# Second mixer of a two-block network: value matrices as stationary operand, three attention branches summed in one PSUM bank

## The chip, the core and the metric

One NeuronCore of a Trainium2 chip runs the whole network for a sequence of 256 tokens of width 2048, batch 1. The time is the device time of one execution in microseconds (us). TensorE (PE), VectorE (DVE), ScalarE (ACT), GpSimd (POOL) and SyncE (SP) each run their own list of instructions in order and wait for each other by semaphores.

## The reference

A first block (pooling and stick-breaking attention, then a feed-forward part) is followed by two mixers. The change is in the last one, `mixer_b`; the first mixer of the pair, `mixer_a`, ends with the same `(o * silu(z)) @ w_out`.

```python
def mixer_b(h, w_in, ..., w_out, cos, sin):
    q, kc, vc, ks, vs, kw, vw, gates, z = jnp.split(h @ w_in, cuts, axis=-1)
    kcmp, vcmp = compress(kc, ...), compress(vc, ...)              # 15 compressed keys and values
    o_cmp, o_slc = nsa_cmp_slc(q, kcmp, vcmp, ks, vs)              # two of the three branches
    o_win = banded_attention(q, kw, vw, B_WINDOW, WIN_QBLOCK)      # the third
    g = jax.nn.sigmoid(gates).reshape(Bn, S, 3, B_KV_GROUPS, B_GROUP, 1)
    o = g[:, :, 0] * o_cmp + g[:, :, 1] * o_slc + g[:, :, 2] * o_win
    return (o.reshape(Bn, S, B_WIDTH) * jax.nn.silu(z)) @ w_out
```

There are 4 key groups of 8 heads with 64 numbers each. At 256 tokens the selected and the window branch both see every earlier token, so both are plain causal softmax attention, with different keys and values.

## The kernel before

Every large product (256 x 2048 times 2048 x N) streams its weights in chunks of 512 columns. One step is one block of 128 rows of a chunk: six matmuls of 512 columns (`mm_tile`, L625 to L627; two token tiles, and three products each, since weights and activations are split into a high and a low fp32r part). The parts are made two steps at a time by `cast` (ACT, L1163, `w_high`) and `rest` (DVE, L1676, `w_low`), three such halves ahead of PE, into rings of four.

The attention rides on this stream. Stage "b" is the list of steps of `b_z` and `b_q` of the four groups and of `b_out`; group g starts at step 32 g, and what hangs on a step stands ahead of that step's six matmuls on PE and ahead of that step's cast and rest on ACT and DVE. Within a group the work goes in eight pairs of heads (pairs 0 to 3 in the selected branch, 4 to 7 in the window branch). Pair i has these pieces, counted in steps from the group's start:

- `pair_scores` (PE, step 8 + 3 i): eight small matmuls into banks 0 and 1.
- `pair_mask` (DVE, same step): adds the mask, two maxima, and the negated maximum.
- `pair_exp` (ACT, step 10 + 3 i): four exponentials, each followed by a read of its row sum.
- `pair_turn` (PE, step 13 + 3 i): six transposes of the weights into banks 1 and 2. It waits until what these banks held has been read.
- `pair_store` (ACT, same step, and ahead of the exponentials that stand on it): one copy of the transposed weights from banks 1 and 2 to `pt`.
- `pair_values` (PE, at the turn of the next pair; for pair 7 at step 37): the transposed weights are the stationary operand and 64 columns of values stream, six matmuls per pair, into bank 3.
- `add_outputs` (DVE, after every second pair): reciprocal of the row sums, times the gate, times the bank (512 columns), added to `oo`.

The compressed branch has its own pieces: `cmp_scores` (PE, step 5), `cmp_shift` and `cmp_weights` (DVE, steps 5 and 7), `cmp_turn` (step 10), and `cmp_values` (PE, step 12), two matmuls of 512 columns into banks 2 and 3 with which `oo_begin` (DVE) starts `oo`. After the last pair `oo_gate` multiplies `oo` by silu(z), and at step 40 (`OO_STEP`) `oo_turn` makes eight transposes on PE, `turn_high` and `turn_low` (L1307 on ACT, L1917 on DVE) split them into `DHI` and `DLO`, the stationary operand of `b_out`.

Stage "a" is the first mixer. It already runs in the form that the change brings to "b": `head_values` (L955, L957) has the values as stationary operand, `z_turn` transposes silu(z) through bank 2, `z_store` (L1488) copies it to `zT`, and `out_gate`, `out_high`, `out_low` finish two heads at a time. It has one pair per six steps.

The scores of a pair write bank 1, so they wait until the turn of two pairs before has been stored:

Of the kernel before, what the change touches and what calls it, by code (L numbers as in the profile page):

```python
# [7 lines left out]
F32 = mybir.dt.float32  # L8
# [5 lines left out]
P = 128  # L14
# [47 lines left out]
    "outputs": ("weights_scaled", "z_turned", "z_stored", "out_gated", "out_high", "out_low", "outputs_read", "branch_added", "rd_step", "oo_gated"),  # L62
# [170 lines left out]
OO_STEP = 40  # L233

Z_STEPS = (18, 23)
# [17 lines left out]
def gate_step(i):  # L253

    return value_step("a", i) + 1
# [15 lines left out]
def body(nc, t, ctx, known):  # L271
# [333 lines left out]
    def tensor_program(T):  # L605
# [298 lines left out]
        def pair_scores(name, g, i, k_):  # L904
# [4 lines left out]
            for tt in range(NT):  # L909
                c0, n = (0, P) if tt == 0 else (P, SEQ)  # L910
                for e in range(2):
                    o = e * HD
                    mm = T.matmul(bank(e)[:, c0:c0 + n], qG[o:o + HD, i % 4, tt * P:(tt + 1) * P], k_[o:o + HD, 0:n],  # L913
                                  start=True, stop=True)
# [15 lines left out]
        def pair_values(name, g, i, vals):  # L930
            if i % 2 == 0:
                T.wait_ge(*emptied[3])
            T.wait_ge(*of("pt_made", (name, g, i)))
            v0, v1 = (vals[:, tt, g * HD:(g + 1) * HD] for tt in range(2))
            for e in range(2):
                s, c0 = 2 * (i % 2) + 1 - e, (2 * (i % 2) + e) * HD
                o0, o1 = bank(3)[:, c0:c0 + HD], bank(3)[:, SEQ + c0:SEQ + c0 + HD]
# [3 lines left out]
            mm.then_inc(*done("valued", (name, g, i)))  # L941
            if i % 2 == 1:
                emptied[3] = of("outputs_read", (name, g, i // 2))

        def oo_turn(g):
            for half in range(2):
                T.wait_ge(*of("oo_gated", ("b", g, half)))
                turn_half("oo_b", g, oo, half, 2)

        def head_values(g, i):  # L950
            T.wait_ge(*emptied[3])
            T.wait_ge(*of("pt_made", ("a", g, i)))
            v0, v1 = (va[:, tt, g * HD:(g + 1) * HD] for tt in range(2))
            for e in range(2):
                T.matmul(bank(3)[e * HD:(e + 1) * HD, 0:SEQ], v0, pt[:, 2 * (i % 2) + 1 - e, 0:SEQ], start=True, stop=False)  # L955
# [1479 lines left out]
```

## Time and profile before

| | us |
|---|---|
| median of 3 runs | 2270.18 |
| lowest and highest run | 2269.04 and 2273.67 |
| the profiled execution, its own time | 2271.82 |
| span of that execution, first to last instruction | 2270.5 |
| PE busy, share of the span | 97% |
| DVE busy, ACT busy | 64%, 48% |

A profile gives start, duration, engine, line and tiles of each instruction, and what an engine was waiting for. The end of a matmul is modelled and reaches into the next one; how much TensorE time a piece takes is read from the starts on both sides of it. A row of a timeline merges equal neighbours ("x6"), and an fp32 matmul that isn't a transpose shows as two records. The engines ACT and DVE begin an instruction while the last part of the one before still runs, so their cost in a row is also the distance of starts.

### The profile page before, as it was taken

What the parts mean: (1) busy time and instruction counts of PE and PEld (TensorE: products, weight loads), DVE (VectorE), ACT (ScalarE), POOL (GpSimd) and SP (SyncE); (2) the same over time, 40 slices, a digit from 0 to 9 for tenths busy, and PEclk for the clock granted to TensorE, in tenths of its full rate; (3) what the DMA queues carried; (4) which work ended last, traced back from release to release, by engine and by line L of the source; (5) the groups of instructions that cost most, each with busy time, mean ns of one, the idle gap of its engine ahead of it and who ended that gap; (6) DMA issues with size and microseconds to landing.
All of it is one profiled execution on the core that took longest, in us unless ns stands there. A gap on an engine that the chain in (4) does not pass through costs nothing.

```text
span 2270.5 us, 27331 instructions
## 1 busy us (share of the span) xinstructions
PE 2206.2 (97%) x10659; PEld 1803.4 (79%) x10659; DVE 1463.9 (64%) x1919; ACT 1078.8 (48%) x1599; POOL 175.9 (8%) x318
## 2 busy tenths in 40 slices
PE   6889999999998999999999999999999999999998
PEld 5777788888887888888888888877778877877777
DVE  6767878888875566565554456566665536666664
ACT  3234356544446534444443544555555524565544
POOL 0004311122210000000000000000000000000000
PEclk8889999999998999999999999999999989999999
DMA  9997866788885677777555555544445633333333
GB/s 344 331 305 271 302 206 230 252 307 304 305 288 164 228 238 238 229 237 226 185 185 192 179 193 178 186 149 149 149 154 185 215 123 126 107 112 113 110 130 130
DMA packets 242165, 468.53 MB, mean 206 GB/s; under 512 B 14363, under 2 KB 52469, under 8 KB 241397
## 3 DMA queue, kind: packets, MB, share of 16 engines
q1 hardware_dynamic: 213552, 387.74, 51.9%
q0 software_dynamic: 20480, 67.13, 8.7%
q10 hardware_dynamic: 8004, 11.93, 1.5%
q8 instruction: 85, 1.39, 0.2%
q14 instruction: 44, 0.35, 0.0%
HBM read 464.65 MB, written 2.10 MB: 206 GB/s over the span
## 4 chain that ended last, share of the span: by engine, by line
PE 88%; DVE 5%; issue 2%; ACT 2%; DMA 2%; POOL 1%; SPq 0%; ACTq 0%; DVEq 0%
PE banks L625 26%; PE banks L627 25%; PE banks L626 25%; PE banks L637 2%; PE banks L913 2%; PE banks L925 1%; DVE ada_acc_vec L1735 1%; DMA ada_w<-in_w_ada 1%; ACT w_high L1163 1%; DVE w_low L1676 1%; PE banks L940 1%; PE banks L939 1%; PE banks L1028 1%; PE banks L938 1%; DVE ada_acc L1696 1%
## 5 line engine op out<-in xcount | busy, mean ns | idle before, releaser
L1676 DVE TENSOR_TENSOR w_low<-raw,w_high 128x1024 fp32r<-128x1024 f32 x674 | 821.9, 1224 | 625.7 <-ACT w_high L1163 625.2
L1163 ACT CAST w_high<-raw 128x1024 fp32r<-128x1024 f32 x674 | 701.4, 1046 | 791.4 <-PE banks L627 791.1
L625 PE MATMUL banks<-w_high,act_a_high 128*128 128x512 f32 (+1 forms) x1696 | 691.2, 408 | 21.7 <-DVE act_a_low L1768 14.2
L626 PE MATMUL banks<-w_low,act_a_high 128*128 128x512 f32 (+1 forms) x1696 | 668.3, 394 | 0.0
L627 PE MATMUL banks<-w_high,act_a_low 128*128 128x512 f32 (+1 forms) x1696 | 668.1, 394 | 0.0
L625 PEld LDWEIGHTS banks<-w_high,act_a_high 128*128 128x128 f32 x1696 | 326.6, 193 | 103.9 <-issue 21.6
L627 PEld LDWEIGHTS banks<-w_high,act_a_low 128*128 128x128 f32 x1696 | 326.3, 192 | 69.5
L626 PEld LDWEIGHTS banks<-w_low,act_a_high 128*128 128x128 f32 x1696 | 326.6, 193 | 63.1 <-issue 2.4
L625 PE MATMUL banks<-w_high,act_b_high 128*128 128x512 f32 x640 | 250.7, 392 | 0.0
L627 PE MATMUL banks<-w_high,act_b_low 128*128 128x512 f32 x640 | 249.1, 389 | 0.0
L626 PE MATMUL banks<-w_low,act_b_high 128*128 128x512 f32 x640 | 249.0, 389 | 0.0
L509 POOL DMA_DIRECT2D ada_w<-in_w_ada x256 | 139.7, 546 | 709.6 <-DVE ada_acc L1696 614.2
L1696 DVE SCALAR_TENSOR_TENSOR ada_acc<-ada_w,cT,ada_acc 128x512 f32<-128x512 f32 x240 | 179.4, 747 | 15.6 <-DMA ada_w<-in_w_ada 12.5
L626 PEld LDWEIGHTS banks<-w_low,act_b_high 128*128 128x128 f32 x640 | 120.2, 188 | 25.1 <-issue 0.5
L627 PEld LDWEIGHTS banks<-w_high,act_b_low 128*128 128x128 f32 x640 | 120.1, 188 | 25.1
L625 PEld LDWEIGHTS banks<-w_high,act_b_high 128*128 128x128 f32 x640 | 120.2, 188 | 25.0 <-issue 0.5
L1471 ACT ACTIVATE scores<-scores,minus_max 128x128 f32<-128x128 f32 x192 | 85.0, 448 | 8.2 <-DVE minus_max L2099 6.7
L1482 ACT COPY ada_w<-banks 128x768 f32<-128x768 f32 x48 | 38.4, 800 | 94.2 <-PE banks L925 94.2
L1735 DVE SCALAR_TENSOR_TENSOR ada_acc_vec<-ada_first,cT,ada_acc_vec 128x512 f32<-128x512 f32 x88 | 66.0, 750 | 4.1 <-DMA ada_first<-in_w_ada 1.8
L625 PE MATMUL banks<-w_high,act_d_high 128*128 128x512 f32 x128 | 51.4, 401 | 1.6 <-DVE act_d_low L1917 1.6
L625 PE MATMUL banks<-w_high,act_c_high 128*128 128x512 f32 x128 | 50.9, 398 | 0.0
L627 PE MATMUL banks<-w_high,act_d_low 128*128 128x512 f32 x128 | 50.0, 391 | 0.0
(338 smaller groups left out, 2013.5 us busy)
## 6 DMA issues: line engine op xcount, KB each, us to landing
raw<-in_w_ff SPq DMA_DIRECT2D x128, 1024.0 KB, 5.2
raw<-in_w_in SPq DMA_DIRECT2D x64, 1024.0 KB, 7.0
ada_w<-in_w_ada POOLq DMA_DIRECT2D x256, 256.0 KB, 4.8
raw<-in_b_w_in SPq DMA_DIRECT2D x44, 1024.0 KB, 5.1
raw<-in_a_w_in SPq DMA_DIRECT2D x36, 1024.0 KB, 5.1
ada_first<-in_w_ada SPq DMA_DIRECT2D x64, 512.0 KB, 9.0
raw<-in_w_o SPq DMA_DIRECT2D x16, 1024.0 KB, 7.1
raw<-in_a_w_out SPq DMA_DIRECT2D x16, 1024.0 KB, 5.2
```

Source lines behind the costliest of these rows:

```text
L509: G.dma_start(ada_w[:, u % ADA_RING, :], t["w_ada"][0, q * P:(q + 1) * P, col:col + AC]).then_inc(*landed(f"ada_landed{u % ADA_RING}", u))
L625: T.matmul(out, xh, wh, start=(c.first and k == 0), stop=False)
L626: T.matmul(out, xh, wl, start=False, stop=False)
L627: last = T.matmul(out, xl, wh, start=False, stop=(c.last and k == c.nk - 1))
L637: tr = T.transpose(bank(b)[:, j * SEQ + tt * P:j * SEQ + (tt + 1) * P], src[:, tt, c0 + j * P:c0 + (j + 1) * P], ident[:, :])
L913: mm = T.matmul(bank(e)[:, c0:c0 + n], qG[o:o + HD, i % 4, tt * P:(tt + 1) * P], k_[o:o + HD, 0:n], start=True, stop=True)
L1163: A.copy(WH[:, h % SPL, :, :], split_ap(h)).then_inc(*done("high", h))
L1471: A.activation(sc[:, s, c0:c0 + n], sc[:, s, c0:c0 + n], ACT.Exp, scale=R, bias=nm[:, i // 4, j, tt:tt + 1], accum_out=sm[:, i // 4, j, tt ...
L1482: A.copy(pt[:, 2 * (i % 2):2 * (i % 2) + 2, :], banks[:, 5:7, 0:3 * P]).then_inc(*done("pt_made", (name, g, i)))
L1676: V.tensor_tensor(WL[:, h % SPL, :, :], split_ap(h), WH[:, h % SPL, :, :].bitcast(F32), ALU.subtract).then_inc(*done("low", h))
L1696: V.scalar_tensor_tensor(out=acc_, in0=w, scalar=c_, in1=acc_, op0=ALU.mult, op1=ALU.add).then_inc(*done("ada_acc", u))
L1735: V.scalar_tensor_tensor(out=acc_, in0=w, scalar=c_, in1=acc_, op0=ALU.mult, op1=ALU.add).then_inc(*done("first_vec", (i, u, kk)))
```

## The change

The output of a pair of heads is now built transposed, in bank 3, for all three branches: the compressed branch first (`vbd` stationary, 256 columns of `cpt` moving), then the selected branch, then the window branch, by accumulation. For that the pairs alternate between the branches (pair 2 j selected, pair 2 j + 1 window), and each branch's weights are scaled by gate over row sum before they are transposed: `gate_factor` on DVE (reciprocal, product, and the first 128 columns of two heads), `pair_scale` on ACT (the other 256 columns of each head). `cmp_values`, `oo_begin`, `add_outputs`, `oo_gate` and the turn of `oo` go; z is transposed instead, at steps 18 and 21, and the outputs are gated and split two heads at a time. On DVE the mask of the next pair stands one step earlier, behind the factor. On ACT the exponentials stand one step earlier.

```diff
@@
-OO_STEP = 40
+EXP = {"a": 2, "b": 1}
+BRANCHES = {"a": 1, "b": 2}
-Z_STEPS = (18, 23)
+Z_STEPS = {"a": (18, 23), "b": (18, 21)}
@@ tensor_program
         def pair_turn(name, g, i):
             for b in (1, 2):
                 T.wait_ge(*emptied[b])
-            T.wait_ge(*of("weights_scaled" if name == "a" else "scores_exp", (name, g, i)))
+            T.wait_ge(*of("weights_scaled", (name, g, i)))
+            if name == "b":
+                T.wait_ge(*of("weights_wide", (name, g, i)))
@@
         def pair_values(name, g, i, vals):
-            if i % 2 == 0:
+            j, first, last = i // BRANCHES[name], i % BRANCHES[name] == 0, (i + 1) % BRANCHES[name] == 0
+            if first:
                 T.wait_ge(*emptied[3])
+            if first and name == "b":
+                T.wait_ge(*of("cpt_made", g))
+                T.matmul(bank(3)[:, 0:SEQ], vbd[0:HB, g, j * P:(j + 1) * P], cpt[0:HB, :, :].rearrange("p a n -> p (a n)"),
+                         start=True, stop=False)
...
-                T.matmul(o0, pt[:, s, 0:P], v0, start=True, stop=True)
-                T.matmul(o1, pt[:, s, P:2 * P], v0, start=True, stop=False)
-                mm = T.matmul(o1, pt[:, s, 2 * P:3 * P], v1, start=False, stop=True)
+                T.matmul(bank(3)[e * HD:(e + 1) * HD, 0:SEQ], v0, pt[:, 2 * (i % 2) + 1 - e, 0:SEQ],
+                         start=(name == "a"), stop=False)
+            for e in range(2):
+                mm = T.matmul(bank(3)[e * HD:(e + 1) * HD, P:SEQ], v1, pt[:, 2 * (i % 2) + 1 - e, 2 * P:3 * P],
+                              start=False, stop=last)
...
+        def z_turn(name, g, half):
+            T.wait_ge(*of("pair_free", (name + "_z", g)))
+            if emptied[2] is not None:
+                T.wait_ge(*emptied[2])
+            transposes(2, zs, 2 * half * P).then_inc(*done("z_turned", (name, g, half)))
+            emptied[2] = of("z_stored", (name, g, half))
@@ scalar_program
+        def pair_scale(g, i):
+            A.wait_ge(*of("rd_step", ("b", g, i, 1)))
+            for e in range(2):
+                w = sc[:, 2 * (i % 2) + e, P:3 * P]
+                A.activation(w, w, ACT.Copy, scale=rd[:, 2 * (i % 4) + e, 1:2]).then_inc(*done("weights_wide", ("b", g, i)))
@@ pair_hooks of ACT
+            for j in range(GH // 2):
+                if rel == gate_step(name, j):
+                    out_high(name, g, j, CHI if name == "a" else DHI)
...
+            for i in range(PAIRS[name]):
+                if rel == score_step(name, i) + EXP[name]:
+                    pair_exp(name, g, i)
+            for i in range(PAIRS[name]):
+                if name == "b" and rel == score_step(name, i) + 2:
+                    pair_scale(g, i)
             for i in range(PAIRS[name]):
                 if rel == turn_step(name, i):
                     pair_store(name, g, i)
-            for i in range(PAIRS[name]):
-                if rel == score_step(name, i) + 2:
-                    pair_exp(name, g, i)
-            if name == "a" and rel in Z_STEPS:
-                z_store(g, Z_STEPS.index(rel))
+            if rel in Z_STEPS[name]:
+                z_store(name, g, Z_STEPS[name].index(rel))
@@ vector_program
+        def gate_factor(g, i):
+            br, j, o, s = i % 2, 2 * (i // 2), 2 * (i % 4), 2 * (i % 2)
+            hs, g0 = slice(o, o + 2), 32 * (br + 1) + GH * g + j
+            V.wait_ge(*of("scores_exp", ("b", g, i)))
+            V.reciprocal(rd[:, hs, :], sm[:, br, j:j + 2, :]).then_inc(*done("rd_step", ("b", g, i, 0)))
...
+            V.tensor_tensor(rd[:, hs, :], rd[:, hs, :], gts[:, :, g0:g0 + 2].rearrange("p a h -> p h a"),
+                            ALU.mult).then_inc(*done("rd_step", ("b", g, i, 1)))
...
+            V.tensor_tensor(w, w, rd[:, hs, 0].unsqueeze(2).broadcast_to([P, 2, P]), ALU.mult).then_inc(*done("weights_scaled", ("b", g, i)))
@@
+                out_hooks("b", g, rel)
                 if rel == 5:
                     cmp_shift(g)
                 if rel == 7:
                     cmp_weights(g)
-                if rel == 12:
-                    oo_begin(g)
                 for i in range(PAIRS["b"]):
-                    if rel == score_step("b", i):
+                    if rel + 1 == score_step("b", i) + 2:
+                        gate_factor(g, i)
+                for i in range(PAIRS["b"]):
+                    if rel + 1 == score_step("b", i):
                         pair_mask("b", g, i, maskB)
```

What the built program holds on ACT for two pairs around step 16 of a group, before: the store (`ada_w<-banks`), then the exponentials of the pair, then the cast.

```order
L1521 ACTIVATE zs<-banks,inverse_rms 128x512 x2
L1482 COPY ada_w<-banks 128x768
L1471 ACTIVATE scores,row_sum<-scores,minus_max 128x128
L1471 ACTIVATE scores,row_sum<-scores,minus_max 128x256
L1471 ACTIVATE scores,row_sum<-scores,minus_max 128x128
L1471 ACTIVATE scores,row_sum<-scores,minus_max 128x256
L1163 CAST w_high<-raw 128x1024 x2
L1482 COPY ada_w<-banks 128x768
```

The same engine now, from the exponentials of pair 3 (step 18) to the store at step 22. L1449 are the exponentials, L1473 the copy of z, L1140 the cast, L1461 `pair_scale`, L1467 the store, L1477 `out_high`.

```order
L1449 ACTIVATE scores,row_sum<-scores,minus_max 128x256
L1473 COPY z_transposed<-banks 128x512
L1140 CAST w_high<-raw 128x1024
L1461 ACTIVATE scores<-scores,row_rec 128x256 x2
L1467 COPY ada_w<-banks 128x768
L1477 CAST act_d_high<-outputs_gated 128x256
L1140 CAST w_high<-raw 128x1024
L1449 ACTIVATE scores,row_sum<-scores,minus_max 128x128
L1449 ACTIVATE scores,row_sum<-scores,minus_max 128x256
L1449 ACTIVATE scores,row_sum<-scores,minus_max 128x128
L1449 ACTIVATE scores,row_sum<-scores,minus_max 128x256
L1473 COPY z_transposed<-banks 128x512
```

The store of pair i - 1 now stands behind the exponentials and the scaling of pair i; the copy of z stands behind the exponentials of pairs 3 and 4, and the second one also behind `out_high` and a cast.

On PE a turn with the values behind it read as follows, before:

```order
L925 MATMUL banks<-ident,scores 128x128 x6
L938 MATMUL banks<-b_values_win,ada_w 128x64
L939 MATMUL banks<-b_values_win,ada_w 128x64
L940 MATMUL banks<-b_values_win,ada_w 128x64
L938 MATMUL banks<-b_values_win,ada_w 128x64
L939 MATMUL banks<-b_values_win,ada_w 128x64
L940 MATMUL banks<-b_values_win,ada_w 128x64
```

And now, where a new pair of heads begins (L940 is the compressed branch, at every second pair):

```order
L929 MATMUL banks<-ident,scores 128x128 x6
L940 MATMUL banks<-ada_w,gate_b 128x256
L945 MATMUL banks<-ada_w,b_values_sel 64x256 x2
L948 MATMUL banks<-ada_w,b_values_sel 64x128 x2
```

On DVE, at steps 19 to 21: mask and maxima of pair 4, then the gating of the first two heads, the rest, the low part, and the factor of pair 4.

```order
L2077 TENSOR_TENSOR scores<-banks,mask_causal 128x768
L2080 TENSOR_REDUCE row_max<-scores 128x2
L2081 TENSOR_REDUCE row_max<-scores 128x2
L2088 TENSOR_SCALAR minus_max<-row_max 128x4
L2100 TENSOR_TENSOR outputs_gated<-banks,z_transposed 128x256
L1662 TENSOR_TENSOR w_low<-raw,w_high 128x1024
L2107 TENSOR_TENSOR act_d_low<-outputs_gated,act_d_high 128x256
L2316 RECIPROCAL row_rec<-row_sum 128x4
L2318 TENSOR_TENSOR row_rec<-row_rec,b_gates 128x4
L2322 TENSOR_TENSOR scores<-scores,row_rec 128x2x128
```

The gating on DVE stands behind a mask that waits for scores, so `out_high` on ACT, and the exponentials behind it, come after that mask too.

## Rows read from the trace of the kernel before

**Rows 1.** The page: busy time by engine.
```profile
PE 2206.2 (97%) x10659; PEld 1803.4 (79%) x10659; DVE 1463.9 (64%) x1919; ACT 1078.8 (48%) x1599; POOL 175.9 (8%) x318
```

**Rows 2.** Stretches: length, busy us (x instructions) by engine, granted clock, DMA share, GB/s.
```profile
1994.12:2071.34 77.22, 76.52 (x456) 60.95 (x455) 51.58 (x89) 42.41 (x102) 0.00 (x0) 0.98 0.35 109
...
2047.80:2051.20 3.40, 3.40 (x46) 3.27 (x44) 1.23 (x1) 0.00 (x0) 0.00 (x0) 1.00 0.54 152
2051.20:2054.60 3.40, 3.40 (x8) 2.64 (x9) 3.16 (x11) 0.95 (x2) 0.00 (x0) 0.51 0.66 252
```

**Rows 3.** Waits of PE, from 1750 us on: us in total, times, longest.
```profile
PE banks L925 <- issue: 2.7, 4, 1.1
PE banks L625 <- DVE act_d_low L1917: 1.6, 1, 1.6
PE banks L938 <- DVE ada_acc L2338: 1.4, 3, 0.5
```

**Rows 4.** Timeline of PE around a turn and values in "b": start, us.
```profile
1921.07 0.39 PE L627 MATMUL banks<-w_high,act_a_low 128*128 128x512 f32 x1
...
1921.95 0.33 PE L938 MATMUL banks<-b_values_sel,ada_w 128*128 128x64 f32 x2
...
1923.53 0.39 PE L626 MATMUL banks<-w_low,act_a_high 128*128 128x512 f32 x1
```

**Rows 5.** Timeline of PE around a turn and values in "a".
```profile
1502.20 0.39 PE L627 MATMUL banks<-w_high,act_a_low 128*128 128x512 f32 x1
...
1503.17 0.65 PE L955 MATMUL banks<-ada_w,gate_b 128*64 128x256 f32 x4
...
1504.31 0.39 PE L626 MATMUL banks<-w_low,act_a_high 128*128 128x512 f32 x1
```

**Rows 6.** Timeline of PE: the records of one `cmp_values`.
```profile
1987.58 1.88 PE L1127 MATMUL banks<-gate_b,ada_w 120*128 120x512 f32 x4
```

**Rows 7.** Timeline of PE: scores, the next turn, the next scores.
```profile
1994.12 0.93 PE L913 MATMUL banks<-mask_window,qG 64*128 64x128 f32 x8
...
1997.86 0.82 PE L925 MATMUL banks<-ident,scores 128*128 128x128 f32 x6
...
2001.34 0.93 PE L913 MATMUL banks<-mask_window,qG 64*128 64x128 f32 x8
```

**Rows 8.** Timeline of DVE: the mask that waited for the first of these scores.
```profile
1995.10 0.96 DVE L2091 TENSOR_TENSOR scores<-banks,mask_causal 128x768 f32<-128x768 f32 x1 [1.38 <-PE banks L913]
...
1997.14 0.17 DVE L2102 TENSOR_SCALAR minus_max<-row_max 128x4 f32<-128x4 f32 x1
```

**Rows 9.** Timeline of ACT: a store, the exponentials of a pair, a cast.
```profile
2027.62 0.80 ACT L1482 COPY ada_w<-banks 128x768 f32<-128x768 f32 x1 [3.38 <-PE banks L925]
2028.32 0.41 ACT L1471 ACTIVATE scores<-scores,minus_max 128x128 f32<-128x128 f32 x1
...
2030.08 1.03 ACT L1163 CAST w_high<-raw 128x1024 fp32r<-128x1024 f32 x1
```

**Rows 10.** Timeline of ACT: the tanh of z.
```profile
1998.06 1.27 ACT L1521 ACTIVATE zs<-banks,inverse_rms 128x512 f32<-128x512 f32 x2 [1.72 <-PE banks L627]
```

**Rows 11.** Groups of ACT in stage "a", 1500 to 1690 us: busy us, mean ns.
```profile
L1492 ACT CAST act_c_high<-outputs_gated 128x256 fp32r<-128x256 f32 x14 | 5.7, 409 | 17.9 <-DVE outputs_gated L2126 17.9
...
L1488 ACT COPY z_transposed<-banks 128x512 f32<-128x512 f32 x6 | 3.5, 582 | 3.9 <-PE banks L637 3.9
```

**Rows 12.** Groups of DVE in stage "a", the same stretch.
```profile
L2126 DVE TENSOR_TENSOR outputs_gated<-banks,z_transposed 128x256 f32<-128x256 f32 x14 | 5.8, 417 | 0.0
```

**Rows 13.** Timeline of DVE: reciprocal and product of `add_outputs`; `cmp_weights` and what follows it.
```profile
1976.28 0.19 DVE L2332 RECIPROCAL row_rec<-row_sum 128x8 f32<-128x8 f32 x1
...
1976.71 0.69 DVE L2338 TENSOR_TENSOR ada_acc<-banks,gate_rec 128x512 f32<-128x512 f32 x1
...
1980.19 0.40 DVE L2317 TENSOR_REDUCE cmp_max<-ada_w 128x16 f32<-128x240 f32 x1
...
1981.65 1.28 DVE L1917 TENSOR_TENSOR act_d_low<-banks,act_d_high 128x512 fp32r<-128x512 f32 x2
```

More of the change, by code:

```diff
@@ L912, in pair_scores @@
                     o = e * HD
[L913 removed]
+                    mm = T.matmul(bank(e)[:, c0:c0 + n], qG[o:o + HD, i // BRANCHES[name], tt * P:(tt + 1) * P], k_[o:o + HD, 0:n],
                                   start=True, stop=True)
@@ L1120, in cmp_turn @@
             emptied[3] = of("cpt_made", g)
-        def cmp_values(g):
-            for b in (2, 3):
-                T.wait_ge(*emptied[b])
-            T.wait_ge(*of("cpt_made", g))
-            for tt in range(NT):
-                mm = T.matmul(bank(2 + tt), cpt[0:HB, tt, :], vbd[0:HB, g, :], start=True, stop=True)
-            mm.then_inc(*done("cmp_valued", g))
-            for b in (2, 3):
-                emptied[b] = of("oo_begun", (g, b - 2))
         for s, (c, k) in enumerate(stage_steps(C, "b")):
@@ L1482, in pair_store, with z_store, out_high @@
             A.copy(pt[:, 2 * (i % 2):2 * (i % 2) + 2, :], banks[:, 5:7, 0:3 * P]).then_inc(*done("pt_made", (name, g, i)))
[L1484 removed]
+        def z_store(name, g, half):
             if g > 0 and half == 0:
[L1486 to L1499 removed]
+                A.wait_ge(*of("out_gated", (name, g - 1, GH // 2 - 1)))
+            A.wait_ge(*of("z_turned", (name, g, half)))
+            A.copy(zT[:, 2 * half:2 * half + 2, :], two(bank(2))).then_inc(*done("z_stored", (name, g, half)))
+        def out_high(name, g, j, H):
+            A.wait_ge(*of("out_gated", (name, g, j)))
+            A.copy(H[:, GH // 2 * g + j, :], gated[:, j % 2, :]).then_inc(*done("out_high", (name, g, j)))
+        def pair_hooks(name, g, rel):
+            for j in range(GH // 2):
+                if rel == gate_step(name, j):
+                    out_high(name, g, j, CHI if name == "a" else DHI)
             if rel == 1:
@@ L2107, in silu @@
                                    op1=ALU.mult).then_inc(*done("pair_free", (name + "_z", g)))
-        def oo_gate(name, g, half, ready_):
-            cols = slice(SEQ * half, SEQ * (half + 1))
-            V.wait_ge(*of("pair_free", (name + "_z", g)))
-            V.wait_ge(*ready_)
-            for tt in range(NT):
-                V.scalar_tensor_tensor(out=oo[:, tt, cols], in0=oo[:, tt, cols], scalar=rh[:, tt:tt + 1], in1=zs[:, tt, cols],
-                                       op0=ALU.mult, op1=ALU.mult).then_inc(*done("oo_gated", (name, g, half)))
@@ new lines, in out_low, with out_hooks @@
+        def out_low(name, g, j):
+            H, L = (CHI, CLO) if name == "a" else (DHI, DLO)
+            k = GH // 2 * g + j
+            V.wait_ge(*of("out_high", (name, g, j)))
+            V.tensor_tensor(L[:, k, :], gated[:, j % 2, :], H[:, k, :].bitcast(F32),
+                            ALU.subtract).then_inc(*done("out_low", (name, g, j)))
+        def out_hooks(name, g, rel):
+            for j in range(GH // 2):
+                if rel == gate_step(name, j):
+                    out_gate(name, g, j)
+                if rel == gate_step(name, j) + 1:
+                    out_low(name, g, j)
@@ L2276, in vector_program @@
         V.wait_ge(*of("pair_free", ("b_gates",)))
-        V.tensor_scalar(gts[:, :, :], gts[:, :, :], 0.5, 0.5, ALU.mult, ALU.add).then_inc(*done("gates_made"))
+        V.tensor_scalar(gts[:, :, :], gts[:, :, :], 0.5, 0.5, ALU.mult, ALU.add).then_inc(*done("gates_made", 0))
+        V.wait_ge(*of("gates_made", 0))
+        for tt in range(NT):
+            V.tensor_scalar(gts[:, tt, :], gts[:, tt, :], rh[:, tt:tt + 1], None, ALU.mult).then_inc(*done("gates_made", 1))
+        V.wait_ge(*of("gates_made", 1))
         for k in range(KT):
```

134 lines of the change are left out of this document (30 added, 104 removed).

## The prediction

> **What bounds the kernel now.** The page comes first: PE is busy 97% of the span [rows 1]. Then the stretch from the first scores of one group of the second mixer to those of the next: 77.2 us, of which PE is busy 76.5 [rows 2]; the other two such stretches are 76.5 us each. DVE has work for two thirds of it and ACT for 55%. So time is gained by taking TensorE work away, and is lost wherever PE, which runs its list in order, meets something that isn't ready. The waits of PE say that it hardly ever does: 2.7 us before turns, 1.4 us before values and 1.6 us at the end of the stage, 5.7 us in 520 [rows 3]. The third question is how much room these waits have, since the change puts more work between a pair's scores and its stored weights.
>
> **What goes, on PE.** Values and turn in "b": from the last matmul ahead (1921.07) to the second one behind (1923.53) are 2.46 us; two stream matmuls of 0.227 are in that, so turn and values take 2.00 us, 0.65 of them the turn (1921.95 - 1921.07 - 0.23) [rows 4]. Stage "a" has the new form: 1504.31 - 1502.20 - 0.45 = 1.66 us [rows 5]. Per pair 0.34 us less; 32 pairs give 10.9 us. The compressed branch: four records of 512 columns per group [rows 6] become four matmuls, thus eight records, of 256 columns, the same number of columns: nothing. It might cost less or more by its weight loads; with half a record (0.2 us) either way per group that is 1 us in the range. The turn of `oo` (eight transposes) is replaced by two turns of z of four: nothing. The existing waits: before values, since bank 3 was read only after a reciprocal and a product (0.43 us [rows 13]) and a 0.69 us multiplication, now one of 0.42 [rows 12]; at the end of the stage, since the outputs of the last heads are split by step 39 and not at step 40; before the first turn of a group, since DVE no longer has two additions, two gatings and a split of 512 columns ahead of its mask. I take all 5.7 us [rows 3] and, since PE loses some 0.2 us more than the idle time shown when it is held up (the next weight load isn't under way), 1.7 us for the eight of them. **Gain: 10.9 + 5.7 + 1.7 = 18.3 us.**
>
> Outside PE: on DVE the factor (0.43 and one multiplication of 0.4) per pair replaces work of the same size per two pairs; on ACT two activations of 256 columns per pair are new. None shows in these rows at that size from SBUF; `out_high` is 0.41 for 256 columns [rows 11], of which about 0.1 overlaps the next, so 0.32 each, bounds 0.3 and 0.5. Neither engine gets full: ACT has for one pair 1.76 + 0.65 + 0.7 + 1.5 x 0.94 = 4.5 us of some 6.9.
>
> **What is put in the way.** I follow one pair. Zero is its first score matmul. DVE masks from 0.98 [rows 7, 8], the negated maximum is there at 3.2 (1997.14 + 0.17), and ACT is on the exponentials until 3.2 + 1.76 = 4.96 [rows 9]. The reciprocal and the product take until 5.5 [rows 13], scaling until 6.15, and only then comes the store of the pair before, 0.8 us [rows 9]: 7.0. The scores of the next pair write bank 1 and wait for that store. On PE they are due after 7.22 us as it was [rows 7], 0.34 less now, so at 6.87; where a new pair of heads starts, 0.43 later (the compressed matmul), at 7.3. Before the change the store stood ahead of the exponentials and was done soon after the turn, which had 3.5 us of room. Now the room is zero, and whatever stands between exponentials and store on ACT goes into PE:
>
> - scores of pair 2. The turn of pair 0 has no values behind it, so they are due at 3.74 + 0.65 + 1.38 = 5.8. On ACT a cast (0.94) comes between, and the mask of pair 1 is late by some 0.85, since it stands behind the factor of pair 0, and that pair's mask behind `cmp_weights` (1.46 us [rows 13]) and a rest. Store done at 7.0 + 0.94 - 0.45 (the cast covers the wait for the factor) + 0.85 = 8.2: **2.4 us**.
> - scores of pair 3: the tanh of z, 1.2 us [rows 10], less 0.5: 7.6 against 7.3: **0.3**.
> - turn of pair 2: bank 2 is held by the z turned at step 18, and `z_store` is behind the exponentials of pair 3: 4.96 + 0.58 [rows 11] + 0.05 = 5.6. The turn is due at 3.74 + 0.43 = 4.2 [rows 7]: **1.4**.
> - turn of pair 3, the same at step 21, but ACT first has `out_high`, which waits for a gating that DVE does behind the mask (3.1 + 0.4 = 3.5), then 0.32 and a cast of 0.94: the exponentials start at 4.8, the copy is done at 7.2, against 4.2: **3.0**.
> - scores of pair 6: a cast between: 7.4 against 6.87: **0.5**.
> - scores of pair 7: `out_high` and cast ahead of the exponentials as above, start 4.8; store done at 8.55 against 7.3: **1.25**.
>
> That is 8.85 us per group; in the first group DVE has nothing left from a group before, 0.8 us less. **Loss: 4 x 8.85 - 0.8 = 34.6 us.** Each of the 24 waits is known to some 0.3 us, bounds 28 and 42.
>
> [...]
>
> [...]
>
> **Sum.** Span 2270.5 - 18.3 + 34.6 + 3.0 = 2289.8. The profiled run's own time is 1.3 us above its span and 1.6 above the median, so the median to expect is 2270.2 + 19.3 = **2289 us**, 0.8% slower. What a measurement can tell from no change here is 0.2%, 4.5 us.
>
> **Rivals.**
> (B) Only the copies of z hold PE up; the scores don't wait. That needs a chain from scores to store shorter by 0.5 to 1 us, for instance if the scaling activations take far under 0.3 us. Then -18.3 + 4 x 4.4 = -0.7: 2269.5. Against it: the store's place on ACT is certain, and 7.0 against 6.87 leaves nothing.
> (C) PE hardly waits at all, the change gives its 18.3 us: 2252. For it: the profile of before has room on every engine. Against: z's copy is behind exponentials that can't begin before 3.2.
> [...]
> (E) The change doesn't save its 0.34 us per pair, since a full-width matmul (compressed branch) now comes between transposes and column-tiled values, and switching costs (1503.17 - 1502.97 = 0.2 us after the last transpose [rows 5]): gain 7 us instead of 18: 2300.
>
> **How the numbers follow.** Forecast (waits of both kinds) 0.58, its own range 2280 to 2298; B 0.12; C 0.09; D 0.13; E 0.08. Slower by over 0.2%: forecast, D, E: 0.79. Within 0.2%: B, 0.12. Faster: C, 0.09. The range takes in B and leaves out C below, and most of what is beyond D above: 2266 to 2305.
>
> **What would show it.** In the profile after: the values in the new form at 1.0 us per pair and no wait before values or at the end of the stage (gain right). Idle of PE before the transposes of the turn, ended by ACT's copy to `z_transposed`, eight times, about 17 us; idle of PE before score matmuls, ended by ACT's store, about 17 us, the longest 2.4 at pair 2 of each group (loss right). Distance from the first scores of a group to the next: about 81 us instead of 77. Wrong if the store is seen done before PE gets to the next scores: then the exponentials or the scaling are shorter than 1.76 and 0.65. Clock: drops near the turns of pair 3, more than one in stage "b".

## The result and the profile after

| | before | after |
|---|---|---|
| median of 4 runs each | 2269.6 | 2295.1 |
| lowest and highest run | 2268.8, 2273.7 | 2289.3, 2299.4 |
| profiled execution, its span | 2271.8, 2270.5 | 2297.2, 2295.9 |

The change makes the kernel slower: ratio 1.0104, interval 1.0088 to 1.0119. The forecast was 2289 us, 2266 to 2305. The four times of after lie 10 us apart, and go in the main with the mean granted clock of each run: 0.979 at 2299.4, 0.978 at 2297.2, 0.982 at 2293.0, 0.985 at 2289.3.

The page of after, busy time by engine:

```profile
PE 2204.0 (96%) x10547; PEld 1782.3 (78%) x10547; DVE 1459.1 (64%) x1953; ACT 1108.2 (48%) x1679; POOL 175.8 (8%) x318
```

PE has 112 records fewer than in [rows 1], yet its busy time fell by 2.2 us only. Where the rest went is seen in the stretch from the first scores of stage "b" to the last pair's scores, first of before, then of after (length, busy us by engine, granted clock, DMA share, GB/s):

```profile
1904.13:2183.97 279.84, 275.76 (x1648) 218.50 (x1647) 188.20 (x322) 155.86 (x379) 0.00 (x0) 0.99 0.34 110
```
```profile
1901.09:2212.39 311.30, 276.01 (x1553) 200.69 (x1553) 186.78 (x361) 184.30 (x457) 0.00 (x0) 0.96 0.30 99
```

The stretch grew by 31.5 us. PE is idle for 35.3 us of it where it was idle for 4.1, and its busy time stayed the same with 95 records fewer, since the mean clock is 0.96. After the last scores 3.0 us are gained (83.5 against 86.5), and the stage begins 3.0 us earlier (1901.1 instead of 1904.1) by things that the change doesn't touch, 1.7 of them since one low stretch of the clock (0.50) near 690 us was 3.4 us shorter in this execution. The waits of PE in after, from 1750 us on (us in total, times, longest):

```profile
PE banks L915 <- issue: 18.0, 14, 2.3
PE banks L929 <- issue: 16.8, 8, 2.9
...
PE banks L940 <- DVE outputs_gated L2100: 0.2, 1, 0.2
```

The three waits of [rows 3] are gone. L915 are the scores, L929 the transposes of the turn. "issue" names no releaser, so each kind has to be followed on ACT. The turn of pair 3 in the last group, on PE:

```profile
2187.44 0.60 PE L639 MATMUL banks<-ident,zs 128*128 128x128 f32 x4
...
2189.03 0.40 PE L629 MATMUL banks<-w_high,act_d_low 128*128 128x512 f32 x1
2192.36 0.84 PE L929 MATMUL banks<-ident,scores 128*128 128x128 f32 x6 [2.93 <-issue]
```

ACT at the same time:

```profile
2188.67 0.41 ACT L1477 CAST act_d_high<-outputs_gated 128x256 fp32r<-128x256 f32 x1 [4.39 <-DVE outputs_gated L2100]
2188.99 1.04 ACT L1140 CAST w_high<-raw 128x1024 fp32r<-128x1024 f32 x1
2189.93 0.40 ACT L1449 ACTIVATE scores<-scores,minus_max 128x128 f32<-128x128 f32 x1
...
2191.70 0.56 ACT L1473 COPY z_transposed<-banks 128x512 f32<-128x512 f32 x1
2192.23 0.91 ACT L1461 ACTIVATE scores<-scores,row_rec 128x256 f32<-128x256 f32 x2
2193.24 0.80 ACT L1467 COPY ada_w<-banks 128x768 f32<-128x768 f32 x1
```

and DVE, where the gating stands behind the mask that waited for the scores:

```profile
2186.07 0.96 DVE L2077 TENSOR_TENSOR scores<-banks,mask_causal 128x768 f32<-128x768 f32 x1 [2.03 <-PE banks L915]
...
2188.22 0.42 DVE L2100 TENSOR_TENSOR outputs_gated<-banks,z_transposed 128x256 f32<-128x256 f32 x1
```

z was transposed at 2187.44, but ACT stood waiting for VectorE's gating (4.39 us idle), then cast, then did the four exponentials, and copied z only at 2191.70; the turn starts 0.1 us after the copy's end. The scores of pair 2 wait for the store (L1467) in the same way; PE and then ACT, in the same group:

```profile
2162.96 0.82 PE L929 MATMUL banks<-ident,scores 128*128 128x128 f32 x6
...
2167.50 1.65 PE L915 MATMUL banks<-mask_window,qG 64*128 64x128 f32 x8 [2.33 <-issue]
```
```profile
2163.11 0.40 ACT L1449 ACTIVATE scores<-scores,minus_max 128x128 f32<-128x128 f32 x1 [0.73 <-DVE minus_max L2088]
...
2164.88 1.03 ACT L1140 CAST w_high<-raw 128x1024 fp32r<-128x1024 f32 x1
2165.82 0.90 ACT L1461 ACTIVATE scores<-scores,row_rec 128x256 f32<-128x256 f32 x2
2166.63 0.78 ACT L1467 COPY ada_w<-banks 128x768 f32<-128x768 f32 x1
```

Turned at 2162.96, stored at 2167.41, scores at 2167.50. And the eight score records take 1.65 us here, where those of [rows 7] take 0.93: the clock has fallen. Three low stretches of the clock, each at the end of a long wait or just behind it, and for comparison the two at and behind the wait of 2.93 us in the last group, where it didn't fall (2024.0 to 2027.4 is low too):

```profile
1938.60:1942.00 3.40, 3.40 (x14) 1.93 (x13) 0.00 (x0) 1.89 (x3) 0.00 (x0) 0.51 0.80 290
2020.60:2024.00 3.40, 2.75 (x10) 1.97 (x12) 0.77 (x3) 2.63 (x6) 0.00 (x0) 0.50 0.80 236
...
2082.10:2085.50 3.40, 3.40 (x13) 2.36 (x14) 1.80 (x3) 0.74 (x1) 0.00 (x0) 0.51 0.81 251
2189.40:2192.80 3.40, 0.47 (x5) 0.47 (x5) 2.32 (x5) 3.40 (x12) 0.00 (x0) 1.00 0.07 6
2192.80:2196.20 3.40, 3.40 (x24) 2.21 (x24) 0.00 (x0) 2.09 (x3) 0.00 (x0) 1.00 0.83 307
```

Busy for all 3.40 us, PE gets 13 or 14 records done at 0.51, and 24 at 1.00. The stage has about 24 us at the low level; before it had 3.4 [rows 2].

### The profile page after: what moved, and what is told of

Same layout as the page of the kernel before. It is cut to its first block, busy times and chain, and to the rows that moved or that the text cites. A ratio compares the mean times of both kernels' runs of the same rounds, so it can differ in the third digit from the quotient of the medians.

```text
span 2295.9 us, 27238 instructions
## 1 busy us (share of the span) xinstructions
PE 2204.0 (96%) x10547; PEld 1782.3 (78%) x10547; DVE 1459.1 (64%) x1953; ACT 1108.2 (48%) x1679; POOL 175.8 (8%) x318
## 4 chain that ended last, share of the span: by engine, by line
PE 83%; DVE 7%; issue 4%; ACT 3%; DMA 2%; POOL 1%; SPq 0%; ACTq 0%; DVEq 0%
PE banks L627 25%; PE banks L629 24%; PE banks L628 24%; PE banks L639 2%; PE banks L915 2%; DMA ada_w<-in_w_ada 1%; ACT w_high L1140 1%; DVE ada_acc_vec L1721 1%; DVE w_low L1662 1%; PE banks L929 1%; PE banks L945 1%; ACT scores L1449 1%; PE banks L1017 1%; SPq L470 0%; DVE ada_acc L1682 0%
## 5 line engine op out<-in xcount | busy, mean ns | idle before, releaser
L1140 ACT CAST w_high<-raw 128x1024 fp32r<-128x1024 f32 x674 | 701.6, 1046 | 769.7 <-PE banks L629 769.2
L627 PE MATMUL banks<-w_high,act_a_high 128*128 128x512 f32 (+1 forms) x1696 | 691.7, 408 | 20.5 <-DVE act_a_low L1754 13.4
L1449 ACT ACTIVATE scores<-scores,minus_max 128x128 f32<-128x128 f32 x192 | 85.0, 444 | 102.8 <-DVE minus_max L2088 68.0
L2077 DVE TENSOR_TENSOR scores<-banks,mask_causal 128x768 f32<-128x768 f32 x32 | 30.6, 955 | 58.8 <-PE banks L915 58.8
L929 PE MATMUL banks<-ident,scores 128*128 128x128 f32 x288 | 40.9, 279 | 17.5 <-issue 16.8
L929 PEld LDWEIGHTS banks<-ident,scores 128*128 128x128 f32 x288 | 34.4, 143 | 27.0 <-issue 22.3
```

Source lines behind the costliest of these rows:

```text
L627: T.matmul(out, xh, wh, start=(c.first and k == 0), stop=False)
L929: tr = T.transpose(bank(2 - e)[:, q * P:(q + 1) * P], sc[:, 2 * (i % 2) + e, q * P:(q + 1) * P], ident[:, :])
L1140: A.copy(WH[:, h % SPL, :, :], split_ap(h)).then_inc(*done("high", h))
L1449: A.activation(sc[:, s, c0:c0 + n], sc[:, s, c0:c0 + n], ACT.Exp, scale=R, bias=nm[:, br, j, tt:tt + 1], accum_out=sm[:, br, j, tt:tt + 1] ...
```

## The experiments

The theory: two kinds of wait, both made by the place of the exponentials on ACT (ahead of the store and of the copy of z) together with the longer chain from scores to scaled weights, and behind the longest of them a lower clock. Against it stand: the new form of the values costs the time (E); the order alone does; the waits are one lateness handed on; the low clock has nothing to do with the waits. Medians here are over 4 to 10 runs. The ratios are to before on the same chip; before itself took 2269.6 beside after and 2270.6 to 2271.9 beside the experiments, so a difference between two kernels that were timed on different chips is known to some 2 us.

**Store first.** The order part of the change undone on ACT; the values, the factor and the scaling stay.

```diff
-EXP = {"a": 2, "b": 1}
+EXP = {"a": 2, "b": 2}
@@ pair_hooks of ACT: pair_store now stands ahead of pair_exp
+                if rel == turn_step(name, i):
+                    pair_store(name, g, i)
+            for i in range(PAIRS[name]):
                 if rel == score_step(name, i) + EXP[name]:
                     pair_exp(name, g, i)
```

> The changed kernel with one part of the edit undone: in the second mixer ScalarE's list holds, for one step, the store of the pair turned before, then the exponentials, then the scaling, then the copy of z; the exponentials thus come a step later in the list than in the changed kernel. Nothing else differs. Theory (ScalarE's order makes the waits): no score waits for the store and the turn of pair 2 no longer waits, 16.8 us of waits before scores and 5.2 of the 18 before turns gone; the turn of pair 3 still waits for the second copy of z, about 1.2 us, four times. So 2295 - 17 - 5 - 7 (turns of pair 3) - some 7 of the lost clock = about 2258, range 2250 to 2265. Rival 1 (the column-tiled values and the change of width on TensorE cost the time, the waits are only where it shows): the time stays within 8 us of 2295. Rival 2 (the clock falls anyway, by the thin columns of turn and values): waits gone, but clock drops in the second mixer stay, about 2265 to 2270.

Measured: 2273.7 us (ratio 1.0014, 1.0005 to 1.0024): 21 us of the 25 are back, but it is 16 us above what was expected. The waits of its PE in the stage:

```profile
PE banks L929 <- issue: 9.4, 4, 2.4
PE banks L940 <- DVE outputs_gated L2100: 4.4, 7, 1.1
PE banks L929 <- DVE scores L2077: 1.2, 4, 0.3
```

All waits before scores are gone, and that of the turn of pair 2. The turn of pair 3 waits 2.35 us and not 1.2. ACT shows why, and the expectation had left it out:

```profile
1935.10 0.40 ACT L1477 CAST act_d_high<-outputs_gated 128x256 fp32r<-128x256 f32 x1 [3.14 <-DVE outputs_gated L2100]
1935.41 1.04 ACT L1140 CAST w_high<-raw 128x1024 fp32r<-128x1024 f32 x1
1936.35 0.58 ACT L1473 COPY z_transposed<-banks 128x512 f32<-128x512 f32 x1
```

No exponential stands here, but ACT still waits for the gating, which VectorE does after the mask of the next pair. The new second row is the same gating: bank 3 isn't free for the next compressed matmul (L940). Three low stretches of the clock, each at the turn of pair 3, remain (0.50 from 1938.50 to 1940.20 in the first). E isn't decided by this alone; the last kernels settle it.

**Copy of z first.** z_store ahead of the exponentials; nothing else.

```diff
         def pair_hooks(name, g, rel):
+            if rel in Z_STEPS[name]:
+                z_store(name, g, Z_STEPS[name].index(rel))
             ...
-            if rel in Z_STEPS[name]:
-                z_store(name, g, Z_STEPS[name].index(rel))
```

> The changed kernel, with ScalarE's copy of z moved ahead of the exponentials of the same step; nothing else differs. Theory: the turn of pair 2 no longer waits (5.2 us), the turn of pair 3 waits 1.2 instead of 2.9 us (6.8 us), the waits of the scores for the store stay at about 17 us or grow by up to 0.3 us each where the copy now stands ahead (pairs 3 and 4): 2295 - 12 - up to 5 of the clock + 2 = about 2280, range 2274 to 2286. If the waits of turns and scores were one and the same lateness handed on from one to the next, taking one kind away would leave the sum as it is, and the time would stay within 4 us of 2295.

Measured: 2282.8 us. Waits: 19.3 before scores (16 times), 4.6 before the turn (4 times, 1.2). As expected in both kinds: the turn's share can be taken away alone, while the scores' stays (1.3 us more). They are two waits, not one handed on.

**Waits filled.** Dummy matmuls from activations that are there, into bank 0, in the time of two of the waits.

```diff
         def pair_turn(name, g, i):
+            if name == "b" and i == 3:
+                T.wait_ge(*emptied[0])
+                fill(12)
@@ pair_scores
+            if name == "b" and i == 2:
+                T.wait_ge(*emptied[0])
+                fill(8)
```

> The changed kernel with dummy matmuls added, whose result nobody reads: in the second mixer TensorE does 8 matmuls of 512 columns into bank 0 just ahead of the scores of pair 2 and 12 just ahead of the turn of pair 3 of each group, in time in which it stood idle in the changed kernel (1.7 to 2.3 and 2.9 us). If such a matmul takes 0.22 us, 8 take 1.8 and 12 take 2.6 us. Theory (the clock falls behind these waits): with the waits filled the clock stays up there, the 9 us that the low clock costs in the second mixer shrink to at most 3, so 2287 to 2290, and the repeats lie closer together than the 10 us of the changed kernel. If the low clock is not tied to the idle time (but to the narrow columns behind it), 2295 or up to 4 us more.

Measured: 2288.8 us (2286.8 to 2289.1, 2.3 us apart), as expected: 80 matmuls more, and 6.2 us less. The same stretch as above, and one filled wait on PE:

```profile
1901.93:2204.22 302.29, 284.16 (x1633) 209.31 (x1633) 186.90 (x361) 184.31 (x457) 0.00 (x0) 1.00 0.31 101
```
```profile
2099.33 2.90 PE L926 MATMUL banks<-act_a_high 128*128 128x512 f32 x12
2102.43 0.85 PE L939 MATMUL banks<-ident,scores 128*128 128x128 f32 x6 [0.20 <-issue]
```

The clock is 1.00 throughout. In after the six transposes of that same turn took longer, with the clock at the low level:

```profile
2106.94 1.51 PE L929 MATMUL banks<-ident,scores 128*128 128x128 f32 x6 [2.91 <-issue]
```

So these low stretches are tied to PE standing idle there. Filling the waits gives back 6.2 us in the median; by the two profiled executions the stage is 9.0 us shorter (311.3 - 302.3).

**z turned together.** As "store first", and both halves of z at step 18, the first through bank 1, the second through bank 2.

```diff
-Z_STEPS = {"a": (18, 23), "b": (18, 21)}
+Z_STEPS = {"a": (18, 23), "b": (18,)}
@@ z_turn
-            if emptied[2] is not None:
-                T.wait_ge(*emptied[2])
-            transposes(2, zs, 2 * half * P)...
+            b = 2 if name == "a" else 1 + half
+            transposes(b, zs, 2 * half * P)...
```

> The changed kernel with the order of e1_store_first, and both halves of z turned at one step (18), the first into bank 1 and the second into bank 2, and copied together; pair 3 then finds both banks long free. Theory: no wait of TensorE above 0.2 us is left in the second mixer, and the gain of the values (0.34 us for each of 32 pairs, and most of the 5.7 us of old waits) is all there: 2252, range 2247 to 2257, faster than both kernels and some 5 us below e1_store_first. If two copies in a row on ScalarE push the exponentials of that step back, a wait of some 0.5 us at the scores of the next pair shows, 2 us in all. Rival (the values did not become cheaper in the whole): 2262 or more.

Measured: 2263.1 us (ratio 0.9970, 0.9957 to 0.9982), faster than both kernels but 11 us above what was expected, in the range that was to speak for the rival. The waits speak against the rival and for a missed third kind:

```profile
PE banks L940 <- DVE outputs_gated L2101: 5.6, 11, 1.1
PE banks L639 <- DVE scores L2078: 1.4, 4, 0.3
PE banks L929 <- DVE scores L2078: 1.2, 4, 0.3
```

8.2 us in 19 waits. The longest, 1.13 us, comes where VectorE rotates the next queries ahead of the gating:

```profile
1961.81 0.29 DVE L2050 TENSOR_TENSOR rope_tmp<-qr,sin_sin 128x128 f32<-128x128 f32 x1 [0.54 <-ACT qr L1424]
...
1963.14 0.42 DVE L2101 TENSOR_TENSOR outputs_gated<-banks,z_transposed 128x256 f32<-128x256 f32 x1
```

**Gating a step earlier**, first on top of "z turned together", then alone on after. It moves on VectorE ahead of the mask of the next scores:

```diff
-                if rel == gate_step(name, j):
+                if rel + (name == "b") == gate_step(name, j):
                     out_gate(name, g, j)
```

> The kernel of e4_z_together with VectorE's gating of the finished heads (in the second mixer) moved one step up in its list: ahead of the mask of the next scores and of one subtraction, and so ahead of the rotation of the next queries. Nothing else differs. In e4_z_together TensorE waits 5.6 us (11 times, up to 1.13) before the compressed matmul for this gating, and 2.6 us (8 times, 0.3 us) for the mask. Theory (the gain of the values is 10.9 us and that of the old waits 7.4 us, and what e4_z_together lacks of it went into these waits): without them 5.6 + 11 x 0.2 us come back, 2263.1 - 7.5 = about 2256, range 2253 to 2259; the waits for the mask stay. If the mask, now 0.4 us later, holds up the scores or turns, 2260. If the gain of the values is smaller than 10.9 us, the waits go and the time stays above 2260 all the same.

Measured: 2255.0 us (ratio 0.9926, 0.9907 to 0.9944), 8.1 us less than without it and as expected; L940 waits no more, the two rows of 0.3 us stay. The gain of the values was there and had gone into these waits.

> The changed kernel with only this edit: VectorE gates the finished heads (second mixer) one step earlier in its list, ahead of the mask. The forecast put 1.6 of the 3.0 us of the turn of pair 3, and the wait at the scores of pair 7, down to ScalarE, which waits for this gating ahead of its exponentials. Theory: turn of pair 3 waits 1.3 to 1.4 us instead of 2.9, scores of pair 7 at most 0.2 instead of 1.45; the others (1.3 at the turn of pair 2, 2.3 at the scores of pair 2) stay. 4 x (1.5 + 1.3) = 11 us of waits less and about 6 us of the low clock: 2295 - 17 = 2278, range 2273 to 2285. If ScalarE isn't held by the gating, nothing changes: 2295, within 4 us.

Measured: 2277.7 us, as expected. PE waits 11.7 us before scores (9 times) and 10.5 before turns (8 times, at most 1.3); the wait at pair 7 is gone, those of 1.3 and 2.3 stay. The forecast put 1.6 us down to ACT held by the gating (3.0 against 1.4); measured are 2.91 - 1.31 = 1.6. In the last group ACT now begins the exponentials when the mask allows it, and the copy comes 1.8 us behind that:

```profile
2172.35 0.40 ACT L1449 ACTIVATE scores<-scores,minus_max 128x128 f32<-128x128 f32 x1 [2.01 <-DVE minus_max L2088]
...
2174.12 0.56 ACT L1473 COPY z_transposed<-banks 128x512 f32<-128x512 f32 x1
```

**No scaling on ACT.**

```diff
-            if name == "b":
-                T.wait_ge(*of("weights_wide", (name, g, i)))
@@ pair_hooks of ACT
-                    pair_scale(g, i)
+                    pass
```

> The changed kernel without the scaling by ScalarE of the wide part of the weights (128x256, two activations per pair) in the second mixer; the output thus lacks the factor there. Order and all else as in the changed kernel. Theory (what stands between exponentials and store on ScalarE goes into the wait of the scores): the activations took 0.9 us and the wait for the factor 0.45; the store can go out some 1.1 us earlier, so the scores of pair 2 wait about 1.2 instead of 2.3 us, those of pair 7 0.3 instead of 1.45, those of pairs 3 and 6 nothing; the turns of pairs 2 and 3 still wait 1.3 and 2.9 us. 4 x (1.1 + 0.45 + 0.66 + 1.15) = 13 us less waiting, and some of the low clock: 2295 - 13 - 3 = 2279, range 2274 to 2285. If the scaling isn't on the path, because the exponentials alone hold the store, 2295 within 4 us.

Measured: 2279.7 us, as expected. The scores wait 5.5 us instead of 18.0 (pair 2 1.55, 0.87 in the first group, the rest at most 0.13), the turns 16.9 as in after. So the scaling and its wait for the factor carry 12.5 of the 18.0 us; at pair 2, where a cast stands between exponentials and store, a wait is left that was put at 1.2.

**The kernel before with the new order.** Exponentials one step earlier and ahead of the store, nothing else.

```diff
+                if rel == score_step(name, i) + (2 if name == "a" else 1):
+                    pair_exp(name, g, i)
+            for i in range(PAIRS[name]):
                 if rel == turn_step(name, i):
                     pair_store(name, g, i)
-            for i in range(PAIRS[name]):
-                if rel == score_step(name, i) + 2:
-                    pair_exp(name, g, i)
```

> The kernel before with only ScalarE's order changed as the change does it: in the second mixer the exponentials stand one step earlier, ahead of the store of the pair turned before; weights and gates are as they were. Theory (room): without the factor and the scaling in the chain the exponentials end at about 4.96 us after the scores and the store at 5.8, due at 7.2; only where a cast or the gating comes between, some 0.3 to 0.8 us of waits per group. The time stays within 3 us of 2270.6. So it takes the scaling as well as the order. If the order of ScalarE alone makes the waits, they show here too, about 17 us before scores and a turn: 2285 or more.

Measured: 2277.5 us (ratio 1.0026, 1.0016 to 1.0035), 6.4 us more. Both theories miss; that of room is nearer in kind, but its size was wrong. The waits, and the stretches at the place of the low clock of [rows 2] (the first two follow each other, the others are the same place in the next groups):

```profile
PE banks L913 <- issue: 6.2, 12, 0.7
PE banks L938 <- DVE ada_acc L2338: 2.1, 3, 0.7
```
```profile
1972.60:1976.00 3.40, 3.40 (x43) 3.17 (x43) 1.16 (x6) 0.00 (x0) 0.00 (x0) 1.00 0.53 143
1976.00:1979.40 3.40, 3.40 (x10) 2.62 (x9) 3.10 (x9) 1.45 (x2) 0.00 (x0) 0.50 0.45 173
2054.50:2057.90 3.40, 3.40 (x9) 2.66 (x9) 3.06 (x10) 1.45 (x2) 0.00 (x0) 0.50 0.54 208
2133.00:2136.40 3.40, 3.40 (x9) 2.63 (x10) 3.18 (x11) 1.13 (x2) 0.00 (x0) 0.50 0.67 260
```

1.55 us of waits before scores per group (0.7 at pair 2, where a cast comes between, 0.35 and 0.5) where at most 0.8 were expected. And the clock falls in three of three groups right after values and compressed scores, without a wait there (the nearest, 0.7 us before values, ended 10 us earlier); before it fell in one of three. Waits 6.2 + 0.7 - 2.7 (the old wait at L925 is gone) = 4.2, and two low stretches more at 1.7 each: 7.6, against 6.4 measured. The order alone thus makes 6.2 us of waits before scores, much as after without the scaling has 5.5; it takes the scaling for the 18.0 of after. The 16.8 us before turns have no counterpart here, since this kernel doesn't copy a transposed z in stage "b".

**Store first and gating earlier**, z in two halves as in after.

> The kernel of e1_store_first with VectorE's gating one step earlier in its list; z is turned in two halves at steps 18 and 21 as in the changed kernel. In e1_store_first TensorE still waits 9.4 us (4 times 2.35) at the turn of pair 3 and 4.4 us before the compressed matmul. Theory (the 2.35 us come from ScalarE, which waits for the gating and then casts before it copies z, and not from the copy itself): both kinds go, at most 0.3 us stays at the turn of pair 3, no clock drop in the second mixer: 2273.7 - 9.4 - 4.4 - 2 (restarts) - 3 (clock) = 2255, range 2252 to 2259, so that turning z together is not needed. If the copy of z at step 21 is late by itself (turned 1.8 us before the turn of pair 3, copied in 0.6 us beside a cast), the turn of pair 3 keeps a wait of about 1 us: 2261 to 2264.

Measured: 2253.6 us (ratio 0.9924, 0.9908 to 0.9941). As expected, and as fast as the kernel with z turned together: the late copy of z was ScalarE's wait for the gating. This is after with the store ahead of the exponentials and the gating ahead of the mask, 18 us faster than before and some 41 faster than after. From "store first" it is 20.1 us away by the medians and 19.6 by the stretch (286.0 - 266.4): 13.0 of waits (15.0 - 2.0), 4.8 in three low stretches of the clock, and 1.9 that PE loses at its waits beyond the idle time shown. Its waits in stage "b" and the stretch of the stage:

```profile
PE banks L929 <- DVE scores L2077: 1.1, 4, 0.3
PE banks L929 <- issue: 0.9, 4, 0.2
```
```profile
1902.34:2168.78 266.44, 264.37 (x1554) 193.82 (x1553) 181.74 (x359) 187.27 (x454) 0.00 (x0) 1.00 0.35 115
```

## Why the prediction was right, point by point

**Gain, 18.3 us predicted.** It is there, and the last kernel shows it nearly free of the losses: 13.4 us in the stretch (279.8 - 266.4) and 3.0 behind it (83.5 instead of 86.5), 16.4; with the 2.0 us that it still waits 18.4. That 18.4 falls on 18.3 is in part luck: 1.7 of it is the one low stretch that before had, which the forecast didn't count, and against it stands about as much that the last kernel loses at its eight waits beyond the idle time shown. Turn and values on PE in after, a pair with the compressed matmul:

```profile
1917.60 0.39 PE L629 MATMUL banks<-w_high,act_a_low 128*128 128x512 f32 x1
1917.83 0.82 PE L929 MATMUL banks<-ident,scores 128*128 128x128 f32 x6
1918.48 0.60 PE L940 MATMUL banks<-ada_w,gate_b 120*128 120x256 f32 x2
1919.01 0.65 PE L945 MATMUL banks<-ada_w,b_values_sel 128*64 128x256 f32 x4
...
1920.15 0.40 PE L628 MATMUL banks<-w_low,act_a_high 128*128 128x512 f32 x1
```

By the method of the forecast 1920.15 - 1917.60 - 0.45 = 2.10 us; the same count over the pairs without the compressed matmul gives 1.67, against 2.01 before: 0.34 per pair, as predicted. The compressed branch costs 0.42 for each of 16 matmuls, 6.7 us, against the 7 us that four `cmp_values` took (the records of [rows 6], 1.75 us each time by the distance of starts). The waits of [rows 3] went.

**Waits, 34.6 us predicted, 34.8 measured.** One by one, in us (predicted, measured):

| place | predicted | after |
|---|---|---|
| scores of pair 2 | 2.4 | 2.33 (1.67 in the first group) |
| scores of pair 3 | 0.3 | 0.45 in two groups, none where the clock had fallen at pair 2 |
| turn of pair 2 | 1.4 | 1.28 to 1.31 |
| turn of pair 3 | 3.0 | 2.90 to 2.93 |
| scores of pair 6 | 0.5 | 0.66 to 0.67 |
| scores of pair 7 | 1.25 | 1.44 to 1.47 |

Both causes were tested one at a time: the gating ahead of the exponentials (1.6 of the 3.0), the scaling ahead of the store. The chain to the scores of pair 2 holds link by link, with two errors that cancel. In the last group, counted from the first scores of pair 1 (2159.23), the exponentials begin at 3.88 (4.05 by the forecast), the two scalings take 0.81 us by the distance of starts (0.65), and the store is done at 8.18 (8.2).

What the forecast left out on this side is what it counted on the gain's, the time that PE loses beyond the idle time shown. A turn of pair 2 takes 3.17 us with 1.31 idle where one without a wait takes 1.67, so 0.19 more; at the scores it is 0.07. Over 8 turns and 14 scores that is 2.5 us, and the stretch of after has 1.4 us more of it than that of the last kernel. At least a part of it is only how idle time is shown: a matmul's record is 0.39 us long while the starts in the stream lie 0.23 apart, so the idle time shown begins 0.16 us late. In before it is the same: the turn at 1915.41, with 0.23 us of wait shown, starts 0.63 behind the matmul ahead of it (1914.78), 0.17 more than the wait and the 0.23 of the stream. The next weight load isn't under way in a wait, as the forecast had it: ahead of the wait of 2.93 us it starts at 2192.33, only 0.03 before the first transpose, while at the turn without a wait it starts at 1917.60, 0.23 before. That PE loses time by this, beyond the way idle time is shown, isn't shown.

**Clock, 3.0 us predicted, 10.3 measured in the profiled execution.** This is the term that was mis-sized. No run shows the 3.0, which was the author's estimate of a part of four drops at 1.7 us, half of the 3.40 us at 0.51 in [rows 2]. What the runs showed in its place: after and the last kernel have the same list on PE, so their starts can be set against each other matmul by matmul: in the five low stretches of the stage after loses, waits left out, 1.6, 2.9, 1.6, 2.7 and 1.6 us, 10.3 in all. Of that 0.9 came back at once, since two waits of 0.45 us before the scores of pair 3 fell away; the filled waits gave back 9.0 by the profiled executions and 6.2 by the medians, the profiled execution of after being 2 us above its median. The place was right (turn of pair 3) and one place was missing (scores of pair 2). The estimate took one chance in three from a place without any wait; in fact the clock fell behind three of four turns of pair 3, twice for twice as long as one stretch, and behind two of four scores of pair 2. Counted over the profiled executions, a low stretch followed 18 of the 24 waits of 1.67 to 2.93 us (after 5 of 8, "store first" 3 of 4, "copy of z first" 4 of 4, "gating alone" 3 of 4, "no scaling" 3 of 4), and none of the shorter ones. Rival D (a drop of 1.7 us behind each of the twelve waits at the turns of pairs 2 and 3 and the scores of pair 2, 2306) had the tie to the waits right, as the filled waits show, and its price per drop fits the single ones (1.6); it overcounted by the turns of pair 2, behind which none fell, and by three of the other eight.

The filled waits are the plain case of a low clock tied to idle time here: at most 0.54 us idle where 1.67 to 2.93 had been, no low stretch, 6.2 us less. The low stretch of before and those of "before with the new order" came without a gap, and no run here shows what brought it.

**Sum.** 2270.5 - 18.3 + 34.6 + 3.0 was 2289.8. The measured terms are -18.4, +35.2 (the waits with three short ones at L940), +1.4 (beyond the idle time shown), +10.3 (clock) and -3.0 (ahead of the stage, by no doing of the change), together +25.5; the two spans differ by 25.4. The forecast's span was 6 us low: the clock took 7.3 more, waits and what hides behind them 2.0 more, and the 3.0 ahead of the stage, which was luck, gave a part back.

**Rivals.** B (only the copies wait) and C (no waits) fell with the 18.0 us before scores. C is the kernel that the change could have been: 2252 predicted, 2253.6 with two places of the order changed. E fell with the gain in full. Of the signs named, the eight waits for the copy (16.8 for "about 17"), those for the store (18.0 for "about 17") and the missing old waits came; the distance of groups is 82.6 to 85.5 us instead of 81, which is the clock again (1.6 to 4.3 us of it per group).

## What to carry to other kernels

When a change puts work between the producer and the consumer of a buffer that the bound engine writes again, follow each link on the helper engines in their own order; ACT, busy for 48% of the span, still made PE wait for a bank for up to 2.93 us. What decided some 41 us here was no operation but two places in two lists: the store behind the exponentials, the gating behind the mask. And after removing a wait, look for what waits next: the same late gating held the copy of z, the exponentials and bank 3, and the last of these was seen only when the other waits were gone.

## What was not expected

- The waits of PE cost more here than their idle time: 34.8 us of them came with 10 us of lower clock and 2.5 us beyond the idle time shown. Work that does nothing, 80 matmuls in two kinds of the waits, made the kernel 6.2 us faster and its four runs agree to 2.3 us instead of 10.
- The same wait of 2.9 us was followed by a low clock in three groups and not in the fourth, so single runs of this kernel can scatter by it (its four lie 10 us apart), and a median over few of them too.
- The clock fell without any wait behind values with 64 moving columns and scores with 15 (0.50 in 1976.0 to 1979.4 of "before with the new order", in all three groups), and at this place in no kernel in which the values have 256 and 128 moving columns. That the values are the reason wasn't tried by itself.
